# Three seven-product units in each gate/up chunk, and a weight sum made by an adding transfer

## The chip, the core and the metric

The kernel runs on one core of a Trainium2 chip. The metric is device time in microseconds of one execution, the median of several; the profile is of one further execution and gives times from the start of its span. The engines are TensorE (PE; its weight loads are shown as PEld), VectorE (DVE), ScalarE (ACT), GpSimd (POOL) and SyncE (SP), which here only issues transfers.

## What is computed

One encoder block on 256 tokens of width 2048 in float32: a gated feed-forward network of width 5632, a mixing stage (sparse attention and a recurrent time mix between two projections), a second network, a last norm. The change lies in the two networks:

```python
def swiglu(x, w_gate, w_up, w_down):
    return (jax.nn.silu(x @ w_gate) * (x @ w_up)) @ w_down

h = h + 0.5 * swiglu(rms_norm(h, ffn1_norm[l]), ffn1_w_gate[l], ffn1_w_up[l], ffn1_w_down[l])
...
h = h + 0.5 * swiglu(rms_norm(h, ffn2_norm[l]), ffn2_w_gate[l], ffn2_w_up[l], ffn2_w_down[l])
```

## The kernel before

**Products.** Each float32 factor is split into a high and a low part, and a product is three matmuls: high by high, high by low, low by high. Weights come in groups of 256 rows by 512 columns (512 KB). For a group, SP loads it into one of four slots of `raw` (`load_group`, L382), ScalarE copies the high part to `whi` (`split_hi`, L396), VectorE subtracts to get the low part in `wlo` (`split_lo`, L404), and PE multiplies it with two blocks of 128 tokens: 2 x 2 x 3 = 12 matmuls with 512 columns (`project_tokens`, L419). `whi` and `wlo` have four slots as well. The load of group g waits until group g-4 has been split by both engines; a split waits until PE has used group g-4.

**Units.** Two groups together, of the gate and of the up matrix (or of two column blocks of the down matrix), make a 2 x 2 by 2 x 2 block product, which needs seven products instead of eight: 21 matmuls instead of 24 (`unit_products`, L433). For that VectorE makes sums of the raw weights in `col_sum` (`unit_sums`, L786): four additions of 128 x 512, one of which replaces the first half of the up group in its raw slot by the sum of its two halves. ScalarE and VectorE split the sums (`unit_hi`, `unit_lo`), and PE takes first the gate group, then the up group, then the sums. `col_sum` and its low part share one buffer, so the sums of a unit wait until PE has finished the unit before (`unit_used`); in the down stage the raw sums have a buffer of their own. Sums of token blocks are made once for each network, beside its first chunk (`halves_dve`, `halves_hi`, `halves_lo`).

**Gate/up stage.** Each network has eleven chunks of 512 columns (`FC`), of 16 groups each. The first has no units. In each of the other ten the order of the groups is written out in `CHUNK` (L47): gate groups into psA, up groups into psB, two units between them; shared partial products of the units go to psT and psM. When they are done, ScalarE copies one share out, VectorE adds the shares (`close_gate`, L929: four instructions on 128 x 512 and one on 128 x 1024), and ScalarE applies silu to psA (`silu_gate`, L702), all near the end of the same chunk. PE may begin the next chunk when silu has read psA. Product of gate and up (`gate_up`, L901), a transpose by quads through DRAM (`turn_quads`, `quads_store`, `quads_load`) and its split (`turned_hi`, `turned_lo`) follow during the next two chunks. SP stores the quads ahead of group 11 and reads them back ahead of group 13.

**Down stage.** Two pairs of column blocks, each with 44 groups; seven units in each pair (seven and eight in the second network), with two plain groups between two units, 14 or 6 plain groups ahead of the first and 4, 10 or 12 behind the last (`down_order`, L83). The same `unit_sums` serves it.

Every engine runs its instructions in the written order. POOL issues some small loads of parameters at the start (L2699), and in the mixing stage it clears three buffers (`mix_pool`, L1236).

Of the kernel before, what the change touches and what calls it, by code (L numbers as in the profile page):

```python
# [19 lines left out]
ALU = mybir.AluOpType  # L20
# [23 lines left out]

GATE_UNITS = 2
GATE_PAIR = 2
CHUNK = ([("gate", j) for j in (0, 1, 4, 5)] + [("unit", 0)] + [("gate", j) for j in (6, 7)] + [("up", 0)] + [("unit", 1)]  # L47
         + [("up", j) for j in (1, 4, 5, 6, 7)])
UNITS = ((7, 7), (7, 8))
# [108 lines left out]
def build(nc, a, out):  # L158
    with ExitStack() as ctx:
# [128 lines left out]
        x_sum_hi = at("x_sum_hi", [P, 3, GATE_UNITS, P], consts, plus=4 * P + 12 * P * GATE_UNITS, dt=F32R)  # L288
        shares = at("shares", [P, TB, COLS], consts, plus=4 * P + 24 * P * GATE_UNITS)
        xl_sum = at("xl_sum", [P, KD, S], xl)  # L290
# [62 lines left out]
        act_lo_ready = sem("act_lo_ready")  # L353
        col_step = sem("col_step")
        col_hi_ready = sem("col_hi_ready")
        col_lo_ready = sem("col_lo_ready")
# [119 lines left out]
        def squares_act(f, c):  # L476

            if f == 0:
                nc.scalar.wait_ge(x_landed[c], 16)
            else:  # L480
                nc.scalar.wait_ge(x_added, DC * (f - 1) + c + 1)
            if f == 2 and c == 0:
                stored(nc.scalar, "pv", 1)
            for tb in range(TB):
                dump = (silu[:, tb, :] if f == 0 else psT[:, tb * COLS:(tb + 1) * COLS] if f == 2 or c == DC - 1
                        else shares[:, tb, :])
# [214 lines left out]
        def ffn_act(f, base, first_act):  # L701
            def silu_gate(n):  # L702
# [12 lines left out]
                last.then_inc(silu_ready, 1)  # L715

            def turned_hi(n):

                nc.scalar.wait_ge(quads_landed, n * 16 + 16 * (f * FC + 1))
                for tb in range(TB):  # L720
                    last = nc.scalar.copy(turned_tokens(hh, n, tb), landed[:, tb])
                last.then_inc(hh_ready, 1)

            def first_chunk():
                for j in range(PER):
                    if j >= SLOTS:
# [4 lines left out]
                    if j == PER - 2:  # L731
                        halves_hi(xh, xl_sum, x_sum_hi, x_sum, GATE_PAIR // 2, sum_number(f))

            def chunk(n):
                for kind, j, g in chunk_items():
                    split_hi(base, n, PER, g)
                    if kind == "unit":
                        unit = FIRST_UNIT[f] - GATE_UNITS + j
                        nc.scalar.wait_ge(col_step, n * (4 * GATE_UNITS) + (4 * unit + 2))
                        split_hi(base, n, PER, g + 1)  # L740
                        unit_hi(n, unit)
                    if g == PER - 2:

                        nc.scalar.wait_ge(quads_stored, n * 64 + 64 * f * FC)
                        nc.scalar.wait_ge(unit_used, n * GATE_UNITS + FIRST_UNIT[f])
                        nc.scalar.copy(silu[:, 0, :], Q1).then_inc(share_copied, 1)
                silu_gate(n)
                turned_hi(n - 1)
            first_chunk()
# [6 lines left out]
            for i, (m, kind, part, j, g) in enumerate(down_items(f)):  # L756
                split_hi(down, 0, 0, g)
                if kind == "unit":
                    nc.scalar.wait_ge(col_step, 4 * unit + 2)
                    split_hi(down, 0, 0, g + 1)  # L760
                    unit_hi(0, unit, col_raw)
                    unit += 1
                if i == GD + SLOTS:
                    turned_hi(FC - 1)
# [14 lines left out]
        def unit_hi(n, unit, col_sum=col_sum):  # L779

            nc.scalar.wait_ge(col_step, n * (4 * GATE_UNITS) + (4 * unit + 4))
# [32 lines left out]
        def batch(b, f):  # L814

            if f is None:
                return 2, slice(0, 2)
            n = min(2, max(UNITS[f]) - 2 * b)
# [81 lines left out]
        def ffn_dve(f, base, first_dve):  # L900
# [40 lines left out]
            def first_chunk():  # L941
                for j in range(PER):
                    if j >= SLOTS:
                        split_lo(base, 0, PER, j)
                    first_dve(j)
                    if j == PER - 3:
                        nc.vector.wait_ge(group_used, base + GD + GATE_PAIR + GATE_UNITS)
                        halves_dve(xh, xl, xl_sum, x_sum, GATE_PAIR // 2, sum_number(f))
                    if j == PER - 1:
                        halves_lo(xh, xl, xl_sum, x_sum_lo, x_sum_hi, x_sum, GATE_PAIR // 2, sum_number(f))  # L950

            def chunk(n):
                for kind, j, g in chunk_items():
                    if kind == "unit":
                        unit = FIRST_UNIT[f] - GATE_UNITS + j
                        unit_sums(base, n, PER, g, unit)
                        split_lo(base, n, PER, g)
# [4 lines left out]
                    else:  # L962
                        split_lo(base, n, PER, g)
                    if g == 1 and not (isinstance(n, int) and n == 1):
                        turned_lo(n - 2)
                    if g == SLOTS - 1:
# [10 lines left out]
            for i, (m, kind, part, j, g) in enumerate(down_items(f)):  # L977
                if kind == "unit":
                    if unit == FIRST_UNIT[f] + GATE_TOTAL:
                        nc.vector.wait_ge(unit_used, unit)  # L980
                    unit_sums(down, 0, 0, g, unit, col_raw)
                    split_lo(down, 0, 0, g)
# [3 lines left out]
                else:  # L986
                    split_lo(down, 0, 0, g)
                if i == 1:
                    turned_lo(FC - 2)
# [26 lines left out]
            if f == 1:  # L1016
                gain_dve(2)

        def add_down(f, down, c):
# [47 lines left out]
        def ffn_pe(f, base):  # L1067
# [22 lines left out]
            def chunk(n):  # L1090

                nc.tensor.wait_ge(silu_ready, n + f * FC)
                for i, (kind, j, g) in enumerate(chunk_items()):
                    if kind == "gate":
                        project_tokens(psA, xh, xl, base, n, PER, g, j * KT, i == 0, False)
                    elif kind == "up":
                        project_tokens(psB, xh, xl, base, n, PER, g, j * KT, j == 0, j == GD - 1, open_half=0)
                    else:
# [335 lines left out]
        def stored(eng, name, i):  # L1434
# [16 lines left out]
        vector_step = sem("vector_step")  # L1451
        count = {}

        def done(ins, name):

            if name in steps:
                ins.then_inc(steps[name], 1)
# [4 lines left out]
        def need(eng, name):  # L1462

            eng.wait_ge(steps[name], 1)

        def after(name):

            if name in steps:
                nc.vector.wait_ge(steps[name], 1)
# [1230 lines left out]
        def _(pool):  # L2700
# [7 lines left out]
            for row, col_, name in ((0, 0, "rwkv_mu_w"), (0, 64, "rwkv_mu_a"), (1, 0, "rwkv_mu_g"), (1, 64, "rwkv_mu_g")):  # L2708
                pool.dma_start(prow2[row:row + 1, col_:col_ + 64], a[name].rearrange("(o n) -> o n", o=1))\
                    .then_inc(const_landed, 16)  # L2710
            mix_pool(pool)

        @block.scalar
# [152 lines left out]
```

## Time and profile before

| | |
|---|---|
| median of 3 runs | 1834.93 us (1834.79 to 1837.94) |
| span of the profiled execution | 1834.2 us |
| PE busy | 1819.6 us, 99%, 10696 matmuls |
| DVE busy | 1505.4 us, 82% |
| ACT busy | 995.2 us, 54% |
| POOL busy | 11.1 us, 1% |
| bytes moved | 380.36 MB, 207 GB/s over the span |

Matmuls are pipelined: a row's duration is longer than the distance to the next row, and the distance is what a matmul costs. On VectorE and ScalarE, too, a row's duration is a little longer than the distance between neighbours that don't wait. A number in brackets at the end of a timeline row is the idle time before it, with what ended it. The first network lies in about the first 630 us of the span, the mixing stage after it up to about 1080 us, then the second network.

### The profile page before, as it was taken

How to read it: one execution, taken by the hardware profiler on the slowest of the kernel's cores; microseconds unless marked ns; L12 is line 12 of the kernel's file. 1: busy time of each engine (PE TensorE's matmuls, PEld its weight loads, DVE VectorE, ACT ScalarE, POOL GpSimd, SP SyncE). 2: the span in 40 equal slices, each digit the busy share in tenths (PEclk: the TensorE clock that was granted, in tenths of full speed). 3: DMA queues.
4: the chain of work that ended last, by engine and by line, in shares of the span. 5: the costliest groups of instructions: out<-in, count | busy, mean ns of one | idle time of the engine just before them, and what ended most of it. 6: DMA issues, size and time to landing. Idle time of an engine off the chain costs nothing. (4 is left out here: it accounts for less than half of the span.)

```text
span 1834.2 us, 29749 instructions
## 1 busy us (share of the span) xinstructions
PE 1819.6 (99%) x10696; PEld 1546.4 (84%) x10696; DVE 1505.4 (82%) x1755; ACT 995.2 (54%) x1181; POOL 11.1 (1%) x23
## 2 busy tenths in 40 slices
PE   9999999999999999999999999999999999999998
PEld 7888888888888888999998878888888888888886
DVE  5888888888988985788867866688888888889996
ACT  7555555545555655754535655545555555555554
POOL 1000000000000000000000000000000000000000
PEclk9999999999999999999999999999999999999999
DMA  7677666777766778564443557677777677676664
GB/s 252 221 219 228 219 216 215 220 229 236 233 202 204 225 224 267 173 184 140 138 116 106 176 171 261 180 232 231 229 224 232 216 227 222 217 240 195 209 208 157
DMA packets 207851, 380.36 MB, mean 207 GB/s; under 512 B 16016, under 2 KB 35728, under 8 KB 207504
## 3 DMA queue, kind: packets, MB, share of 16 engines
q1 hardware_dynamic: 206768, 377.08, 65.7%
q10 hardware_dynamic: 480, 1.97, 0.3%
q8 instruction: 61, 1.00, 0.2%
q14 instruction: 30, 0.25, 0.0%
q0 software_dynamic: 512, 0.06, 0.0%
HBM read 360.19 MB, written 18.87 MB: 207 GB/s over the span
## 5 line engine op out<-in xcount | busy, mean ns | idle before, releaser
L402 ACT CAST whi<-raw 128x1024 fp32r<-128x1024 f32 (+1 forms) x648 | 675.1, 1047 | 700.8 <-DVE raw L1476 189.6
L411 DVE TENSOR_TENSOR wlo<-raw,whi 128x1024 fp32r<-128x1024 f32 (+1 forms) x648 | 771.7, 1212 | 208.4 <-ACT whi L402 194.5
L428 PE MATMUL psA<-whi,xh 128*128 128x512 f32 (+1 forms) x572 | 219.5, 384 | 0.5 <-DVE wlo L411 0.5
L428 PE MATMUL psA<-whi,xl 128*128 128x512 f32 (+1 forms) x572 | 219.2, 383 | 0.0
L428 PE MATMUL psA<-wlo,xh 128*128 128x512 f32 (+1 forms) x572 | 219.1, 383 | 0.0
L428 PE MATMUL psB<-whi,xh 128*128 128x512 f32 x544 | 211.7, 389 | 0.0
L428 PE MATMUL psB<-wlo,xh 128*128 128x512 f32 x544 | 211.6, 389 | 0.0
L428 PE MATMUL psB<-whi,xl 128*128 128x512 f32 x544 | 211.6, 389 | 0.0
L428 PEld LDWEIGHTS psA<-whi,xh 128*128 128x128 f32 x572 | 107.4, 188 | 21.6 <-DVE wlo L411 0.7
L428 PEld LDWEIGHTS psA<-whi,xl 128*128 128x128 f32 x572 | 107.4, 188 | 21.2
L428 PEld LDWEIGHTS psA<-wlo,xh 128*128 128x128 f32 x572 | 107.4, 188 | 21.0
L428 PEld LDWEIGHTS psB<-whi,xl 128*128 128x128 f32 x544 | 102.1, 188 | 21.3
L428 PEld LDWEIGHTS psB<-whi,xh 128*128 128x128 f32 x544 | 102.1, 188 | 21.1
L428 PEld LDWEIGHTS psB<-wlo,xh 128*128 128x128 f32 x544 | 102.1, 188 | 21.1
L1252 PE MATMUL psB<-xh,whi 128*128 128x256 f32 x320 | 92.7, 290 | 0.5 <-DVE wlo L411 0.5
L428 PE MATMUL psA<-whi,hh 128*128 128x512 f32 x236 | 91.8, 389 | 0.0
L428 PE MATMUL psA<-wlo,hh 128*128 128x512 f32 x236 | 91.8, 389 | 0.0
L428 PE MATMUL psA<-whi,hl 128*128 128x512 f32 x236 | 91.8, 389 | 0.0
L1252 PE MATMUL psB<-xh,wlo 128*128 128x256 f32 x320 | 90.5, 283 | 0.0
L1252 PE MATMUL psB<-xl,whi 128*128 128x256 f32 x320 | 90.4, 283 | 0.0
L428 PE MATMUL psB<-whi,hh 128*128 128x512 f32 x220 | 85.7, 390 | 0.0
L428 PE MATMUL psB<-whi,hl 128*128 128x512 f32 x220 | 85.6, 389 | 0.0
(520 smaller groups left out, 3447.3 us busy)
## 6 DMA issues: line engine op xcount, KB each, us to landing
raw<-in_ffn_w_gate SPq DMA_DIRECT2D x176, 512.0 KB, 4.5
raw<-in_ffn_w_up SPq DMA_DIRECT2D x176, 512.0 KB, 4.6
raw<-in_ffn_w_down SPq DMA_DIRECT2D x176, 512.0 KB, 4.6
raw<-in_w_in SPq DMA_DIRECT2D x80, 512.0 KB, 3.6
raw<-in_w_out SPq DMA_DIRECT2D x32, 512.0 KB, 4.2
quads_dram<-stage SPq DMA_DIRECT2D x88, 128.0 KB, 4.2
stage<-quads_dram SPq DMA_DIRECT2D x22, 512.0 KB, 4.3
x<-in_x SPq DMA_DIRECT2D x4, 512.0 KB, 7.5
```

Source lines behind the costliest of these rows:

```text
L402: nc.scalar.copy(whi[:, slot, :, 0:ncol], raw[:, slot, :, 0:ncol]).then_inc(hi_ready, 1)
L411: nc.vector.tensor_tensor(wlo[:, slot, :, 0:ncol], raw[:, slot, :, 0:ncol], whi[:, slot, :, 0:ncol].bitcast(F32), ALU.subtract).then_inc(l ...
L428: mm = nc.tensor.matmul(ps[:, tb, 0:ncol], lhs[:, k0 + t, tok], rhs[:, slot, t, 0:ncol], start=(first and t == 0 and p == 0 and tb != open ...
L1252: mm = nc.tensor.matmul(ps[:, i * S:(i + 1) * S], w[:, slot, t, ct * P:(ct + 1) * P], h[:, k0 + t, :], start=(first and t == 0 and p == 0 ...
```

## The change

A gate/up chunk gets three units instead of two (gate and up rows 2, 3 and 4 of eight), and its order is rewritten: two plain groups between the first unit and the second, one between the second and the third, three behind the third. In all units, those of the down stage too, the sum of the up group's two halves is no longer a VectorE instruction: POOL issues a transfer that reads the second half of the group from DRAM again and adds it to the first half in the raw slot (256 KB, `accum_op`), after the group has landed and after the unit before had its transfer; VectorE's sums and ScalarE's split of the up group wait for it. VectorE's remaining three sums are rearranged. The closing sums of a chunk, with the copy of the share and silu, move behind the first split of the next chunk (in the last chunk, behind the first split of the down stage), and `turned_hi` moves behind the second. `shares` moves into the buffer of `col_sum`. Two groups of four semaphores of the mixing stage become one counted semaphore each.

```diff
-GATE_UNITS = 2
+GATE_UNITS = 3
 GATE_PAIR = 2
-CHUNK = ([("gate", j) for j in (0, 1, 4, 5)] + [("unit", 0)] + [("gate", j) for j in (6, 7)] + [("up", 0)] + [("unit", 1)]
-         + [("up", j) for j in (1, 4, 5, 6, 7)])
+CHUNK = ([("gate", j) for j in (0, 1, 5, 6)] + [("unit", 0), ("gate", 7), ("up", 0), ("unit", 1), ("up", 1), ("unit", 2)]
+         + [("up", j) for j in (5, 6, 7)])
...
+            def copy_share(n):
+
+                nc.scalar.wait_ge(quads_stored, n * 64 + 64 * f * FC)
+                nc.scalar.wait_ge(unit_used, n * GATE_UNITS + FIRST_UNIT[f])
+                nc.scalar.copy(silu[:, 0, :], Q1).then_inc(share_copied, 1)
...
             def chunk(n):
                 for kind, j, g in chunk_items():
                     split_hi(base, n, PER, g)
+                    if g == 0 and not (isinstance(n, int) and n == 1):
+                        copy_share(n - 1)
+                        silu_gate(n - 1)
+                    if g == 1 and not (isinstance(n, int) and n == 1):
+                        turned_hi(n - 2)
                     if kind == "unit":
                         unit = FIRST_UNIT[f] - GATE_UNITS + j
-                        nc.scalar.wait_ge(col_step, n * (4 * GATE_UNITS) + (4 * unit + 2))
+                        wait_summed(nc.scalar, n, unit)
                         split_hi(base, n, PER, g + 1)
                         unit_hi(n, unit)
-                    if g == PER - 2:
-
-                        nc.scalar.wait_ge(quads_stored, n * 64 + 64 * f * FC)
-                        nc.scalar.wait_ge(unit_used, n * GATE_UNITS + FIRST_UNIT[f])
-                        nc.scalar.copy(silu[:, 0, :], Q1).then_inc(share_copied, 1)
-                silu_gate(n)
-                turned_hi(n - 1)
...
+        def wait_summed(eng, n, unit):
+
+            eng.wait_ge(up_summed, n * (16 * GATE_UNITS) + 16 * (unit + 1))
+
+        def sum_rows(pool, n, unit, pair, w, col, base, per, g):
+
+            wait_raw(pool, base + g + 1, n, per)
+            if not (isinstance(n, int) and n * GATE_UNITS + unit == 0):
+                pool.wait_ge(up_summed, n * (16 * GATE_UNITS) + 16 * unit)
+            second = w[(pair * KT + 1) * P:(pair * KT + 2) * P, :]
+            pool.dma_start(raw[:, (base + g + 1) % SLOTS, 0, :], second[:, bass.ds(col, COLS)], accum_op=ALU.add)\
+                .then_inc(up_summed, 16)
+
         def unit_sums(base, n, per, g, unit, col_sum=col_sum):
 
             gate, up = (base + g) % SLOTS, (base + g + 1) % SLOTS
-            steps = n * (4 * GATE_UNITS)
+            steps = n * (3 * GATE_UNITS)
             wait_raw(nc.vector, base + g, n, per)
-            wait_raw(nc.vector, base + g + 1, n, per)
...
-            tt(col_sum[:, 0, :], raw[:, gate, 0, :], raw[:, up, 0, :], ALU.add).then_inc(col_step, 1)
-            nc.vector.wait_ge(col_step, steps + (4 * unit + 1))
-            tt(raw[:, up, 0, :], raw[:, up, 0, :], raw[:, up, 1, :], ALU.add).then_inc(col_step, 1)
-            tt(col_sum[:, 1, :], col_sum[:, 0, :], raw[:, up, 1, :], ALU.add).then_inc(col_step, 1)
-            nc.vector.wait_ge(col_step, steps + (4 * unit + 3))
+            tt(col_sum[:, 1, :], raw[:, gate, 0, :], raw[:, up, 0, :], ALU.add).then_inc(col_step, 1)
+            nc.vector.wait_ge(col_step, steps + (3 * unit + 1))
+            tt(col_sum[:, 0, :], col_sum[:, 1, :], raw[:, up, 1, :], ALU.subtract).then_inc(col_step, 1)
             tt(col_sum[:, 2, :], col_sum[:, 1, :], raw[:, gate, 1, :], ALU.add).then_inc(col_step, 1)
...
             def chunk(n):
                 for kind, j, g in chunk_items():
                     if kind == "unit":
                         unit = FIRST_UNIT[f] - GATE_UNITS + j
+                        wait_summed(nc.vector, n, unit)
                         unit_sums(base, n, PER, g, unit)
...
+                    if g == 0 and not (isinstance(n, int) and n == 1):
+                        close_gate(n - 1)
                     if g == 1 and not (isinstance(n, int) and n == 1):
                         turned_lo(n - 2)
...
-                    if g == PER - 2:
-                        close_gate(n)
...
                 if kind == "unit":
                     if unit == FIRST_UNIT[f] + GATE_TOTAL:
                         nc.vector.wait_ge(unit_used, unit)
+                    wait_summed(nc.vector, 0, unit)
                     unit_sums(down, 0, 0, g, unit, col_raw)
```

## Rows read from the trace of the kernel before

**Rows 1.** The page: busy us, share, instructions; slices of the span in tenths.
```profile
PE 1819.6 (99%) x10696; PEld 1546.4 (84%) x10696; DVE 1505.4 (82%) x1755; ACT 995.2 (54%) x1181; POOL 11.1 (1%) x23
...
PE   9999999999999999999999999999999999999998
...
PEclk9999999999999999999999999999999999999999
```

**Rows 2.** Stretches: length; busy us of PE, PEld, DVE, ACT, POOL; clock, DMA share, GB/s.
```profile
309.11:351.27 42.16, 42.16 (x187) 34.92 (x186) 35.97 (x38) 22.29 (x23) 0.00 (x0) 1.00 0.71 225
478.00:620.00 142.00, 142.00 (x628) 117.64 (x627) 129.57 (x157) 77.52 (x82) 0.00 (x0) 1.00 0.68 213
...
1826.00:1834.00 8.00, 0.86 (x4) 0.38 (x2) 2.32 (x6) 2.26 (x5) 0.00 (x0) 0.71 0.59 221
```

**Rows 3.** Timeline of PE: start, duration; starts of two chunks, then of two down units.
```profile
309.11 0.39 PE L428 MATMUL psA<-whi,xh 128*128 128x512 f32 x1
309.34 0.39 PE L428 MATMUL psA<-wlo,xh 128*128 128x512 f32 x1
...
351.27 0.39 PE L428 MATMUL psA<-whi,xh 128*128 128x512 f32 x1
...
515.83 0.39 PE L439 MATMUL psT<-whi,hh 128*128 128x512 f32 x1
...
526.03 0.39 PE L439 MATMUL psT<-whi,hh 128*128 128x512 f32 x1
```

**Rows 4.** Timeline of DVE around the chunk that PE begins at 309.11.
```profile
303.40 1.23 DVE L411 TENSOR_TENSOR wlo<-raw,whi 128x1024 fp32r<-128x1024 f32 x1 [1.01 <-ACT whi L402]
...
314.18 0.68 DVE L1476 TENSOR_TENSOR col_sum<-raw 128x512 f32<-128x512 f32 x1
...
316.83 2.35 DVE L411 TENSOR_TENSOR wlo<-raw,whi 128x1024 fp32r<-128x1024 f32 x2
319.10 1.75 DVE L1476 TENSOR_TENSOR col_lo<-col_sum,col_hi 128x1536 fp32r<-128x1536 f32 x1
...
327.57 0.69 DVE L1476 TENSOR_TENSOR col_sum<-raw 128x512 f32<-128x512 f32 x1 [2.12 <-DMA raw<-in_ffn_w_up]
...
339.87 0.69 DVE L1476 TENSOR_TENSOR shares<-psM,stage 128x512 f32<-128x512 f32 x1
...
342.51 1.22 DVE L1476 TENSOR_TENSOR shares<-psT,shares 128x1024 f32<-128x1024 f32 x1
```

**Rows 5.** Timeline of ACT in the same chunk: a split; silu and what follows.
```profile
315.69 1.05 ACT L402 CAST whi<-raw 128x1024 fp32r<-128x1024 f32 x1 [2.60 <-DVE raw L1476]
...
342.51 1.27 ACT L714 ACTIVATE stage<-psA,ss 128x512 f32<-128x512 f32 x2 [0.87 <-DVE psA L1476]
343.67 1.14 ACT L721 CAST hh<-stage 128x512 f32 x2
```

**Rows 6.** SP's queue: two issues; landing of L389's loads, 309 to 351.
```profile
318.21 0.37 SPq L389 DMA_DIRECT2D raw<-in_ffn_w_up  x1
319.40 0.37 SPq L389 DMA_DIRECT2D raw<-in_ffn_w_gate  x1
...
DMA to landing us min/median/max: 3.7/4.6/6.1
```

**Rows 7.** Transfers of the whole run: KB each, median us from issue to landing.
```profile
raw<-in_ffn_w_down SPq DMA_DIRECT2D x176, 512.0 KB, 4.6
...
out<-x SPq DMA_DIRECT2D x8, 256.0 KB, 2.5
...
lora_g<-in_rwkv_g ACTq DMA_DIRECT2D x2, 256.0 KB, 4.4
...
prow<-in_mix_norm POOLq DMA_DIRECT2D x1, 8.0 KB, 5.3
```

**Rows 8.** Timeline of DVE in the down stage: first sums of a unit.
```profile
510.07 0.69 DVE L1476 TENSOR_TENSOR col_raw<-raw 128x512 f32<-128x512 f32 x1
...
539.53 0.69 DVE L1476 TENSOR_TENSOR col_raw<-raw 128x512 f32<-128x512 f32 x1 [0.73 <-DMA raw<-in_ffn_w_down]
```

More of the change, by code:

```diff
@@ L288, in build @@
         x_sum_hi = at("x_sum_hi", [P, 3, GATE_UNITS, P], consts, plus=4 * P + 12 * P * GATE_UNITS, dt=F32R)
-        shares = at("shares", [P, TB, COLS], consts, plus=4 * P + 24 * P * GATE_UNITS)
+        shares = at("shares", [P, TB, COLS], col_sum)
+        dump_at = at("dump_at", [P, TB, COLS], consts, plus=4 * P + 12 * COLS)
         xl_sum = at("xl_sum", [P, KD, S], xl)
@@ L354, in build @@
         col_step = sem("col_step")
+        up_summed = sem("up_summed")
         col_hi_ready = sem("col_hi_ready")
@@ L485, in squares_act @@
                 dump = (silu[:, tb, :] if f == 0 else psT[:, tb * COLS:(tb + 1) * COLS] if f == 2 or c == DC - 1
-                        else shares[:, tb, :])
+                        else dump_at[:, tb, :])
                 nc.scalar.activation(dump, x[:, tb, c * COLS:(c + 1) * COLS], ACT.Square,
@@ L730, in first_chunk @@
                         silu_gate(0)
-                    if j == PER - 2:
+                    if j == PER - 1:
                         halves_hi(xh, xl_sum, x_sum_hi, x_sum, GATE_PAIR // 2, sum_number(f))
@@ L758, in ffn_act @@
                 if kind == "unit":
-                    nc.scalar.wait_ge(col_step, 4 * unit + 2)
+                    wait_summed(nc.scalar, 0, unit)
                     split_hi(down, 0, 0, g + 1)
@@ L762, in ffn_act @@
                     unit += 1
+                if i == 0:
+                    copy_share(FC - 1)
+                    silu_gate(FC - 1)
+                if i == 1:
+                    turned_hi(FC - 2)
                 if i == GD + SLOTS:
@@ L779, in unit_hi @@
         def unit_hi(n, unit, col_sum=col_sum):
-            nc.scalar.wait_ge(col_step, n * (4 * GATE_UNITS) + (4 * unit + 4))
+            nc.scalar.wait_ge(col_step, n * (3 * GATE_UNITS) + (3 * unit + 3))
             if not (isinstance(n, int) and n * GATE_UNITS + unit == 0):
@@ L816, in batch @@
             if f is None:
-                return 2, slice(0, 2)
+                return GATE_UNITS, slice(0, GATE_UNITS)
             n = min(2, max(UNITS[f]) - 2 * b)
@@ L945, in first_chunk @@
                     first_dve(j)
-                    if j == PER - 3:
+                    if j == PER - 2:
                         nc.vector.wait_ge(group_used, base + GD + GATE_PAIR + GATE_UNITS)
                         halves_dve(xh, xl, xl_sum, x_sum, GATE_PAIR // 2, sum_number(f))
-                    if j == PER - 1:
-                        halves_lo(xh, xl, xl_sum, x_sum_lo, x_sum_hi, x_sum, GATE_PAIR // 2, sum_number(f))
             def chunk(n):
@@ L963, in chunk @@
                         split_lo(base, n, PER, g)
+                    if g == 0 and not (isinstance(n, int) and n == 1):
+                        close_gate(n - 1)
                     if g == 1 and not (isinstance(n, int) and n == 1):
                         turned_lo(n - 2)
+                    if g == 1 and isinstance(n, int) and n == 1:
+                        halves_lo(xh, xl, xl_sum, x_sum_lo, x_sum_hi, x_sum, GATE_PAIR // 2, sum_number(f))
                     if g == SLOTS - 1:
                         gate_up(n - 1)
-                    if g == PER - 2:
-                        close_gate(n)
             first_chunk()
@@ L987, in ffn_dve @@
                     split_lo(down, 0, 0, g)
+                if i == 0:
+                    close_gate(FC - 1)
                 if i == 1:
@@ L1017, in ffn_dve, with ffn_pool, chunk @@
                 gain_dve(2)
+        def ffn_pool(pool, f, base, w_up, w_down):
+            def chunk(n):
+                for kind, j, g in chunk_items():
+                    if kind == "unit":
+                        sum_rows(pool, n, FIRST_UNIT[f] - GATE_UNITS + j, GATE_PAIR + j, w_up, n * COLS, base, PER, g)
+            chunk(1)
+            with pool.Fori(2, FC) as n:
+                chunk(n)
+            unit = FIRST_UNIT[f] + GATE_TOTAL
+            for m, kind, part, j, g in down_items(f):
+                if kind == "unit":
+                    sum_rows(pool, 0, unit, j, w_down, (2 * m + 1) * COLS, base + FC * PER, 0, g)
+                    unit += 1
         def add_down(f, down, c):
@@ L1092, in chunk @@
                 nc.tensor.wait_ge(silu_ready, n + f * FC)
+                first_up = next(j for kind, j in CHUNK if kind == "up")
                 for i, (kind, j, g) in enumerate(chunk_items()):
@@ L1096, in chunk @@
                     elif kind == "up":
-                        project_tokens(psB, xh, xl, base, n, PER, g, j * KT, j == 0, j == GD - 1, open_half=0)
+                        project_tokens(psB, xh, xl, base, n, PER, g, j * KT, j == first_up, j == GD - 1, open_half=0)
                     else:
@@ L1447, in build @@
             "kr_out", "k_roped", "qi_roped", "q_packed0", "q_packed1", "q0_roped", "q1_roped", "q_back0", "q_back1",
[2 rows of a table removed]
+            "scored0", "scored1", "scored2", "scored3", "max0", "max1", "max2", "max3", "exp",
+            "recip", "shares0", "shares1", "shares2", "shares3",
             "att_hi0", "att_hi1")}
@@ L1452, in build @@
         count = {}
+        counted = {f"{name}{n}": (name, n + 1) for name in ("exp", "recip") for n in range(4)}
         def done(ins, name):
-            if name in steps:
+            if name in counted:
+                ins.then_inc(steps[counted[name][0]], 1)
+            elif name in steps:
                 ins.then_inc(steps[name], 1)
@@ L1462, in need @@
         def need(eng, name):
-            eng.wait_ge(steps[name], 1)
+            name, level = counted.get(name, (name, 1))
+            eng.wait_ge(steps[name], level)
         def after(name):
-            if name in steps:
+            if name in counted:
+                nc.vector.wait_ge(steps[counted[name][0]], counted[name][1])
+            elif name in steps:
                 nc.vector.wait_ge(steps[name], 1)
@@ L2710, in _ @@
                     .then_inc(const_landed, 16)
+            ffn_pool(pool, 0, 0, *ffn1[1:])
             mix_pool(pool)
+            ffn_pool(pool, 1, base2, *ffn2[1:])
         @block.scalar
```

2 rows, old and new, of the table steps are left out of this document.

## The prediction, made before the changed kernel was run

> **What bounds the kernel now.** I read the page's busy shares and slices first, then the busy time of two stretches, then the timelines of PE, VectorE, ScalarE and the SP queue inside one gate/up chunk, last the transfers. PE is busy 99% of the span, in every slice, at the full granted clock [rows 1]. In the gate/up chunk that runs from 309.11 to 351.27 PE never pauses: 42.16 us busy of 42.16, VectorE 35.97, ScalarE 22.29 [rows 2]. Matmuls follow each other every 0.227 us (309.11, 309.34), and one chunk begins 42.16 us after the last [rows 3]: 12 plain groups of 12 matmuls and two units of 21 are 186 matmuls. So a chunk is bound by PE's matmul count alone; a group costs 2.72 us, a unit 4.76 us for two groups. In the down stage it is the same: unit starts lie 10.20 us apart, one unit and two plain groups [rows 3].
>
> What the reader must see next is how little stands between this and another bound. The ring of raw weights has four slots; the load of group g waits until g-4 is split. VectorE finishes the first split of the chunk at 304.63 (303.40 and 1.23), PE wants it at 309.11, so the lead is 4.5 us [rows 3, 4]; ahead of the second unit VectorE already stands 2.12 us still for a load [rows 4], and in the down stage its sums wait for a load too [rows 8].
>
> **What is removed.** Per chunk three matmuls: 183 x 0.2267 = 41.48 us, 0.68 less, in 20 chunks 13.6 us. This is the only work that leaves PE; the down stage keeps its matmuls. VectorE loses one sum per unit: the four sums fill 314.18 to 316.83, 2.65 us [rows 4], so three take 2.0. Its third unit adds 2.0 of sums and 1.67 of low halves (the 1.75 row, less the overlap of neighbours); with 2 x 0.65 off, a chunk is 35.97 + 2.4 = 38.3 us of 41.48. VectorE's throughput does not become the bound. ScalarE gains one 1.4 us copy at 22 of 42 us: hidden, and hidden still if the chunk shortens.
>
> **What is added, and on which path.** The sum of the up rows moves from VectorE, where it followed the landing at once, into a transfer issued by POOL, which must wait for the landing, is issued, reads the rows again, adds, lands; VectorE then begins its sums. VectorE is in order: behind its new wait stand the splits of the unit's gate and up groups, hence the slots' release, hence the next loads of SP. ScalarE's split of the up group waits as well, with the high copy behind it. I call the price of the transfer, from issue to landing, T. The lines of the diff for the down units add the same wait there.
>
> No row shows an adding transfer. The nearest: a plain 256 KB store, 2.5 us with little else moving; a 256 KB load for lora_g, 4.4 us; POOL's own small transfers, 5.3 us, at a time when the engines were crowded [rows 7]. Bounds: 2.5 below (a gain below nothing is excluded, a step that wasn't there can't land before it is issued), above 5.3 plus 0.7 for the bytes, 6.0. I take 4.4, the row of the same size and direction. The Trainium skill (DMA: Bandwidth & Descriptors, "Anatomy of one DMA — SWDGE (gpsimd) path") gives a fixed 2.0 us and bytes over 436 GB/s for POOL's transfers; that would be T = 2.6, an estimate by that page; POOL's 5.3 us for 8 KB here disagree, in a crowded stretch [rows 7].
>
> **The slot's turn.** From the end of one unit's second split to the end of the next unit's in the same slot: to SP's issue 0.15 (the first of two splits ended at about 318.06, issue 318.21 [rows 4, 6]), load L, POOL's and VectorE's wake 0.1 each, T, sums 2.0, two splits 2.3 [rows 4]. That is L + T + 4.65. For L the loads of the chunk took 3.7 at least and 4.6 in the median [rows 6]; of those on this path some go out alone and some behind another, so 4.2.
>
> A chunk after the change has this cycle, all in the order of the queues: group 1 to group 5 (unit 0's up rows), one turn; 5 to 9 (unit 1's), one turn; group 8, split 1.15 earlier, to group 12 (unit 2's), one turn less 1.15; group 12 to the next chunk's group 0, a plain refill of L + 2.55 (0.15, a wake of 0.1, ScalarE's split 1.05, hand-over 0.1, VectorE's 1.15 [rows 4, 5]); then the closing sums, now behind that first split. They hold up group 1: four of the five sums 2.64 (339.87 to 342.51 [rows 4]), silu on ScalarE 1.16 (342.51 to 343.67 [rows 5]), ScalarE's split of group 1, 1.05, VectorE's 1.15, hand-overs 0.3, together 6.3. Sum: 4L + 3T + 21.65. With 4.2 and 4.4 it is 16.8 + 13.2 + 21.65 = 51.65 us against 41.48 of PE: the ring is the new bound. Against 42.16 each chunk loses 9.49 us, 20 chunks 190, less the lead of 4.5 us that each network begins with: 181.
>
> Moving the closing sums by itself is covered: PE wants silu only three plain groups (8.16 us) after the last unit, and copy 0.57, sums 2.64 and silu 1.16 take about 4.7 with hand-overs. If the cover were gone it would cost at most those 4.7 us a chunk; in the cycle above it is counted. SP's stores and load of the turned quads stay at groups 11 and 13, where SP waits longer for splits than for them: nothing. The larger token sums in the first chunk, half as much work again, and the moved low halves lie beside the first chunk's matmuls: nothing to 2 us per network.
>
> **Down stage.** A turn now: VectorE starts its sums every 9.82 us on average (510.07 to 539.53, three turns [rows 8]), just under PE's 10.20, and the load at 4.6 [rows 7] accounts for it: 0.15 + 4.6 + 0.1 + 2.65 + 2.3 = 9.8. After: 9.25 + T = 13.65. 25 gaps between units lose 3.45 each, 86 us; the first units of the four strings, with four plain groups (10.9) ahead of them, 2.75 each, 11; less a lead of 4.5 four times, 18: 79 us.
>
> **Sum.** The profiled span is 1834.2 and the median of the runs 1834.93, 0.7 around it. 1834.9 + 181 + 79 = 2095 us.
>
> **Rivals.** (a) *Faster: PE's 0.68 us count, T is hidden.* 1834.9 - 13.6 = 1821. It decides below 4L + 3T + 21.65 = 41.48, that is T = 1.0 at L = 4.2 and 1.7 at 3.7; every row in [rows 7] speaks against it. A second thing speaks against it even at T = 0: unit 2 follows unit 1 after one plain group (2.72 us), and its sums share one buffer with unit 1's, so they wait for unit 1's last product; sums 2.0, split 1.15 and hand-overs 0.2 are 3.35, a pause of 0.63, which eats the 0.68. Chance 0.03.
> (b) *No change*, T small and that pause cancelling the gain: 1835, chance 0.04.
> (c) *Slower by a third of it: the transfer is quick.* With T = 2.5, at L = 4.2, a chunk is 45.95 (20 x 3.79 - 9 = 67) and a down turn 11.75 (39 + 3 - 18 = 24): 1926. The 2.5 us store [rows 7] speaks for it, POOL's 5.3 against. Chance 0.24. The page of the Trainium skill named above, with its 2.6, would give about this, an estimated 1935.
> (d) *Much slower*: T = 6.0 and L = 4.6, loads and adds in each other's way: chunk 58.05 (20 x 15.89 - 9 = 309), down turn 15.25 (126 + 17 - 18 = 125): 2269. The granted clock, 1.00 through all of this, is 0.71 in the last 8 us, where PE has nearly stopped, so part of them at 1.2 GHz [rows 2]; pauses of several us in a chunk could bring that and would lengthen PE's own part. Chance 0.14.
> My forecast, 1990 to 2180, has 0.55: T from about 3.2 to 5.4 at 89 us for each 1 us.
>
> **Range.** Lowest by the bounds, T = 2.5 and L = 3.7 (4.2 in the down stage): 43.95 a chunk, 27 us, and 13 for the down stage: 1875. Highest 2269. Between them lie the forecast, (c) and (d); outside (a), (b) and the tails. About 0.2% (3.7 us) is what a measurement of this kernel tells from no change: faster 0.03, same 0.04, slower 0.93.
>
> **What would show it.** Right: PE pauses in each gate/up chunk ahead of the units' splits, the chunk near 52 us; VectorE's first sum of a unit ended by the adding transfer, its issue-to-landing near 4.4 us; unit starts in the down stage near 13.7 us apart; loads not slower than now; the mixing stage between the two networks unchanged in length. Wrong: chunks of 42 us with VectorE's wait ended elsewhere (T hidden, so the slots are free earlier than I have it), or chunks that stretch while the adds land within 3 us (then a queue's order, or the clock, and not T). The weakest number is T: each 1 us of it moves the total by 3 x 20 + 29 = 89 us, one for each unit.

## The result, and the profile after

The changed kernel takes 2317.12 us in the median (2309.64 to 2319.55) against 1835.76 before, measured beside it: a ratio of 1.262, 95% interval 1.259 to 1.264. The direction is as forecast; the loss, 481 us, is nearly twice the 260 us forecast and lies above the top of the range. The profiled execution has a span of 2314.0 us. The page after, first busy time and slices (against [rows 1]), then the chain that ended last:

```profile
PE 1972.1 (85%) x10636; PEld 1624.1 (70%) x10636; DVE 1530.2 (66%) x1766; ACT 1009.3 (44%) x1201; POOL 88.3 (4%) x112
...
PE   9788878778797878999999998888878888887877
...
PEclk9988998989898999999999998889899999988999
...
DMA 21%; DVE 7%; PE 7%; issue 6%; ACT 2%; DVEq 0%; ACTq 0%; POOLq 0%; SPq 0%
```

Sixty matmuls are gone (10696 before), as the change says. But PE is no longer busy in every slice, VectorE's share has fallen from 82% to 66%, and the chain runs through transfers for 21% of the span. The slices also show where nothing happened: the middle, the mixing stage, is full as before. Its last projection, the matmuls of one tile with first and last start, takes as long in both kernels, 100.8 and 100.9 us (the first row is of the kernel before, the second of the changed one):

```profile
L428 PE MATMUL psB<-whi,mix_hi x64: 389/389/580, 1029.6 to 1130.4; 128*128 128x512 f32 x64
```

```profile
L430 PE MATMUL psB<-whi,mix_hi x64: 389/389/580, 1264.1 to 1365.0; 128*128 128x512 f32 x64
```

The first matmuls of the down stages (the first start in each row) say in which stages the time went. The first two rows are the first network's, before and after; the other two are the second's:

```profile
L428 PE MATMUL psA<-whi,hh x120: 389/389/389, 477.8 to 656.6; 128*128 128x512 f32 x120
```

```profile
L430 PE MATMUL psA<-whi,hh x120: 389/389/500, 642.4 to 878.7; 128*128 128x512 f32 x120
```

```profile
L428 PE MATMUL psA<-whi,hh x116: 389/389/389, 1597.1 to 1773.7; 128*128 128x512 f32 x116
```

```profile
L430 PE MATMUL psA<-whi,hh x116: 389/389/395, 1997.4 to 2236.8; 128*128 128x512 f32 x116
```

The first down stage begins 165 us later than before, the mixing stage's last projection 235, the second down stage 400, and the span ends 480 later. So the gate/up chunks of the two networks lose 165 and 166 us, the first down stage with the mixing stage 70 (2 of them in the mixing stage), the second down stage 80: 330 and 150, where 181 and 79 were forecast. (The mixing stage lies later than is said above: before the change the first down stage's matmuls end at 707 us and the mixing stage's at 1131.) Who waited for whom in the changed kernel (total us, times, longest):

```profile
DVE col_sum L1523 <- DMA raw<-in_ffn_w_up: 363.8, 60, 8.2
...
PE psT L441 <- DVE wlo L413: 325.7, 89, 6.7
...
DVE col_raw L1523 <- DMA raw<-in_ffn_w_down: 176.2, 27, 8.9
```

VectorE's first sum waits at every unit of the chunks, 60 times, and PE waits once for each of the 89 units, always at a unit's first product, for VectorE's low half of its gate group. The transfers (KB, median us from issue to landing; then least, median and most of the 89 adding ones), against [rows 7]:

```profile
raw<-in_ffn_w_gate SPq DMA_DIRECT2D x176, 512.0 KB, 4.7
raw<-in_ffn_w_up SPq DMA_DIRECT2D x176, 512.0 KB, 4.2
...
raw<-in_ffn_w_up POOLq DMA_DIRECT2D x60, 256.0 KB, 6.1
...
DMA to landing us min/median/max: 4.5/6.0/7.9
```

So T, which I took as 4.4 us, is 6.0. One cycle of the ring, read along the path that the prediction names. SP's issues, the landings of the first load in each of these four rows, then POOL's issues, then VectorE (start, duration):

```profile
350.54 0.37 SPq L391 DMA_DIRECT2D raw<-in_ffn_w_up  x1
...
365.42 4.35 SPq L391 DMA_DIRECT2D raw<-in_ffn_w_up  x2
...
380.66 0.40 SPq L391 DMA_DIRECT2D raw<-in_ffn_w_up  x1
...
394.39 7.80 SPq L391 DMA_DIRECT2D raw<-in_ffn_w_gate  x5
```

```profile
DMA to landing us min/median/max: 3.4/3.4/3.4
...
DMA to landing us min/median/max: 4.6/4.6/4.6
...
DMA to landing us min/median/max: 3.9/3.9/3.9
...
DMA to landing us min/median/max: 4.7/4.7/4.7
```

```profile
354.93 0.86 POOL L807 DMA_DIRECT2D raw<-in_ffn_w_up  x1 [26.24 <-DMA raw<-in_ffn_w_up]
370.70 0.86 POOL L807 DMA_DIRECT2D raw<-in_ffn_w_up  x1 [14.91 <-DMA raw<-in_ffn_w_up]
385.20 0.86 POOL L807 DMA_DIRECT2D raw<-in_ffn_w_up  x1 [13.63 <-DMA raw<-in_ffn_w_up]
```

```profile
349.19 1.22 DVE L413 TENSOR_TENSOR wlo<-raw,whi 128x1024 fp32r<-128x1024 f32 x1 [1.10 <-PE psB L430]
...
360.98 0.69 DVE L1523 TENSOR_TENSOR col_sum<-raw 128x512 f32<-128x512 f32 x1 [4.50 <-DMA raw<-in_ffn_w_up]
...
377.37 0.69 DVE L1523 TENSOR_TENSOR col_sum<-raw 128x512 f32<-128x512 f32 x1 [6.97 <-DMA raw<-in_ffn_w_up]
...
389.87 0.69 DVE L1523 TENSOR_TENSOR col_sum<-raw 128x512 f32<-128x512 f32 x1 [5.40 <-DMA raw<-in_ffn_w_up]
...
400.37 1.23 DVE L413 TENSOR_TENSOR wlo<-raw,whi 128x1024 fp32r<-128x1024 f32 x1 [1.13 <-ACT whi L404]
401.51 0.68 DVE L1523 TENSOR_TENSOR shares<-psM,stage 128x512 f32<-128x512 f32 x1
...
406.49 1.23 DVE L413 TENSOR_TENSOR wlo<-raw,whi 128x1024 fp32r<-128x1024 f32 x1 [1.10 <-ACT whi L404]
```

Group 1 is split from 349.19 on, the next chunk's group 1 from 406.49 on: 57.3 us. Between them: the load of unit 0's up rows goes out at 350.54 and POOL issues the adding transfer at 354.93 (4.4 us), VectorE starts its sums at 360.98 (6.05); unit 1: 365.42, 370.70 (5.3), 377.37 (6.7); unit 2: 380.66, 385.20 (4.5), 389.87 (4.7); the refill of the next chunk's group 0 goes out at 394.39 and is landed 4.7 us later; then the closing sums and silu hold group 1 up. These are 18.9 us that begin with a load, 17.4 that begin with an addition, and 21.0 for the rest.

But the 18.9 hold more than the loads: they landed after 3.4, 4.6, 3.9 and 4.7 us, 16.6 together, and POOL's row begins 1.0, 0.7 and 0.6 us after the landing that it waits for, 2.3 together. The additions landed after 5.8, 6.5 and 4.6 us, 16.9 together, and VectorE's three wakes are the other 0.4. The sum in the prediction had 16.8 for the loads, 0.3 for POOL's hand-over, 13.2 for the additions, 0.3 for VectorE's wakes and 21.05 for the rest. So the cycle has the terms that were forecast, and it is the addition and POOL's hand-over that are longer. It is the same in other chunks: over sixteen of them, worked out from the same rows, the means are 16.6, 2.2, 18.2, 0.4 and 21.06. Nine chunks of the first network, from the first closing sum (110.12) to the tenth (635.87), give 58.4 us each.

### The profile page after: what moved, and what is told of

Its sections match the earlier page's. It is cut to its first block and busy times, and to the rows that moved or that the text cites. A ratio compares the mean times of both kernels' runs of the same rounds, so it can differ in the third digit from the quotient of the medians.

```text
span 2314.0 us, 30169 instructions
## 1 busy us (share of the span) xinstructions
PE 1972.1 (85%) x10636; PEld 1624.1 (70%) x10636; DVE 1530.2 (66%) x1766; ACT 1009.3 (44%) x1201; POOL 88.3 (4%) x112
## 5 line engine op out<-in xcount | busy, mean ns | idle before, releaser
L1523 DVE TENSOR_TENSOR col_sum<-raw 128x512 f32<-128x512 f32 x60 | 41.5, 692 | 363.8 <-DMA raw<-in_ffn_w_up 363.8
L441 PE MATMUL psT<-whi,xh 128*128 128x512 f32 x60 | 39.4, 656 | 226.8 <-DVE wlo L413 226.8
L430 PE MATMUL psA<-wlo,xh 128*128 128x512 f32 (+1 forms) x492 | 188.5, 383 | 0.0
L430 PE MATMUL psA<-whi,xl 128*128 128x512 f32 (+1 forms) x492 | 188.5, 383 | 0.0
L430 PE MATMUL psB<-whi,xh 128*128 128x512 f32 x464 | 180.9, 390 | 0.0
L430 PE MATMUL psB<-wlo,xh 128*128 128x512 f32 x464 | 180.5, 389 | 0.0
L430 PE MATMUL psB<-whi,xl 128*128 128x512 f32 x464 | 180.5, 389 | 0.0
L795 ACT CAST col_hi<-col_sum 128x1536 fp32r<-128x1536 f32 x60 | 88.4, 1473 | 65.6 <-DVE col_sum L1523 65.6
L807 POOL DMA_DIRECT2D raw<-in_ffn_w_up x60 | 52.0, 867 | 1501.7 <-DMA raw<-in_ffn_w_up 1458.4
L1523 DVE TENSOR_TENSOR col_lo<-col_sum,col_hi 128x1536 fp32r<-128x1536 f32 x60 | 105.1, 1751 | 0.0
```

Of the source, the lines that this page charges most:

```text
L430: mm = nc.tensor.matmul(ps[:, tb, 0:ncol], lhs[:, k0 + t, tok], rhs[:, slot, t, 0:ncol], start=(first and t == 0 and p == 0 and tb != open ...
L441: mm = nc.tensor.matmul(into, lhs, rhs, start=(start and p == 0), stop=(stop and p == 2))
L807: pool.dma_start(raw[:, (base + g + 1) % SLOTS, 0, :], second[:, bass.ds(col, COLS)], accum_op=ALU.add)\
L1523: return V.tensor_tensor(out, a0, a1, op)
```

## The experiments

The chunk below is the distance of the closing sums, the mean of nine in the first network.

**Without the adding transfer.** VectorE makes the sum again, all else as changed.

```diff
-                        wait_summed(nc.vector, n, unit)
...
+            tt(raw[:, up, 0, :], raw[:, up, 0, :], raw[:, up, 1, :], ALU.add).then_inc(row_summed, 1)
+            nc.vector.wait_ge(row_summed, n * GATE_UNITS + (unit + 1))
             tt(col_sum[:, 1, :], raw[:, gate, 0, :], raw[:, up, 0, :], ALU.add).then_inc(col_step, 1)
```

> The changed kernel with the one adding transfer per unit taken out: VectorE makes the sum of the up group's halves again (a fourth instruction per unit), everything else as changed: three units per gate/up chunk, closing sums behind the next chunk's first split. Theory (the turn of a raw slot, load + adding transfer + sums + splits, sets the pace, and only the transfer is too long): the chunk goes back from 58.4 us to about 43 to 44 (41.5 of PE, plus the pause of 0.6 to 1.3 us ahead of unit 2, whose sums wait for unit 1), the down stage to its length before, in all 1850 to 1880 us, clock 1.00. Rival A (three units or the moved closing sums make the chunk long): 2100 to 2200 us, since only the down stage, 150 us, comes back.

Measured 1880.35 us, ratio 1.024 (1.022 to 1.025), clock 0.999, chunk 44.2 us (272.28 to 316.30 for one). So 437 of the 481 us are the adding transfer's, and three units with moved closing sums lose 44 us by themselves. Two rows of that run, VectorE's and PE's waits:

```profile
304.16 0.69 DVE L1501 TENSOR_TENSOR raw<-raw 128x512 f32<-128x512 f32 x1 [1.83 <-PE psA L441]
```

```profile
PE psT L441 <- DVE wlo L413: 34.5, 39, 1.4
```

The first sum of unit 2 waits 1.83 us for PE to finish unit 1: rival (a)'s second objection, seen. PE pauses up to 1.4 us, about twice a chunk, and the 0.68 us saved is gone more than once.

**Adding transfers in the down stage alone.**

```diff
+            if col_sum is not col_raw:
+                tt(raw[:, up, 0, :], raw[:, up, 0, :], raw[:, up, 1, :], ALU.add).then_inc(row_summed, 1)
...
-                        wait_summed(nc.vector, n, unit)
...
-                    wait_summed(nc.vector, 0, unit)
+                    wait_added(nc.vector, downs(f, unit))
```

> Adding transfers in the down stage alone; in the gate/up chunks VectorE makes the sum, with three units and moved closing sums as changed. Theory: the two stages lose independently of each other; the chunks as in the run without any adding transfer (44.2 us), the down stage as in the changed kernel, unit starts 15.2 us apart, 29 turns: 1880 + 150 = 2030 us. If the sum of the parts does not hold (2030 missed by more than 20 us), the stages act on each other.

Measured 2030.32 us; chunk 44.2, unit starts in the down stage 15.3 us apart (536.76 to 628.53, six gaps). The stages add up: 150 us in the down stages, the other 287 of the transfer's 437 us in the chunks.

**Two units instead of three, transfer and moved closing kept.**

```diff
-GATE_UNITS = 3
+GATE_UNITS = 2
...
+CHUNK = ([("gate", j) for j in (0, 1, 4, 5)] + [("unit", 0)] + [("gate", j) for j in (6, 7)] + [("up", 0)] + [("unit", 1)]
+         + [("up", j) for j in (1, 4, 5, 6, 7)])
```

> The changed kernel with the old number and order of units, two in a gate/up chunk; adding transfer and moved closing sums stay. Theory: two turns of a slot with the transfer in them instead of three on the path: about 52 us a chunk at a transfer of 6 us, so 20 x 6 us less than changed, about 2180 us, the down stage as changed (unit starts 15.2 us apart). Rival A (the third unit itself is what costs): near 1990 us, only the down stage's 150 us remaining.

Measured 2233.22 us, chunk 54.6 us: the rival falls, but my 2180 us missed too. A turn taken away gave 3.8 us a chunk, not 6. Rows of ScalarE in that run show what I had left out:

```profile
372.63 1.06 ACT L404 CAST whi<-raw 128x1024 fp32r<-128x1024 f32 x1 [2.65 <-PE psB L430]
375.35 1.05 ACT L404 CAST whi<-raw 128x1024 fp32r<-128x1024 f32 x1 [1.66 <-PE psB L430]
```

Behind its last unit this order has five plain groups, and there the splits wait for PE again, which is late by the unit's delay: that part of the path seems to go through PE and not through the ring. This is read from the rows; no run isolates it.

**The parts of the transfer's price.** Three runs change the transfer alone: half the width; a copy instead of an addition; and that copy from ScalarE's queue (in the down stages too, and without the wait for the unit before's transfer).

```diff
-            pool.dma_start(raw[:, (base + g + 1) % SLOTS, 0, :], second[:, bass.ds(col, COLS)], accum_op=ALU.add)\
+            pool.dma_start(raw[:, (base + g + 1) % SLOTS, 0, 0:COLS // 2], second[:, bass.ds(col, COLS // 2)], accum_op=ALU.add)\
```

> The changed kernel with adding transfers of half the width (256 of 512 columns, 128 KB; the sum of the other columns is left out). Its packets are half as long. Theory: about 2.0 us from issue to the first packet stay, the moving time of about 3.5 to 4 us falls; landing 4.5 to 5 instead of 6.0, and each 1 us is worth 3 x 20 + 29 = 89 us: 2190 to 2230 us. Rival (the price is all latency of the software queue): landing near 6, 2300 us. Rival (what costs is the wait's place in VectorE's order, not its length): no change.

```diff
+            pool.dma_start(raw[:, (base + g + 1) % SLOTS, 0, :], second[:, bass.ds(col, COLS)])\
```

> The changed kernel with the same transfers from the same queue, 256 KB each, but copying instead of adding (so the sum is left out: the first half is overwritten by the second). Theory: a packet of 2 KB takes about 85 ns as in the plain loads instead of about 178 ns, the moving time halves: landing about 4.3 us instead of 6.0, 1.7 x 89 = 150 us less, about 2165 us. Rival (the software queue alone costs, adding is free): landing 6, 2300 us.

```diff
                     if kind == "unit":
                         unit = FIRST_UNIT[f] - GATE_UNITS + j
+                        sum_rows(nc.scalar, n, unit, GATE_PAIR + j, w_up, n * COLS, base, PER, g)
                         wait_summed(nc.scalar, n, unit)
```

> As the run with plain copies of 256 KB (no adding, the sum left out), but issued from ScalarE's queue instead of POOL's, right after ScalarE's split of the unit's gate group. Theory: the software queue is a part of the price (about 2 us from issue to first packet); landing about 3.3 us instead of 4.8, 1.5 x 89 = 130 us less than the copies from POOL: about 2070 us. Rival (the queue makes no difference): 2205 us.

Measured 2231.19, 2204.72 and 2172.05 us. The copies landed after 4.8 us where I expected 4.3, and so took 40 us more than the 2165 expected. Landing of the transfers (KB, median), half width, copy, copy from the other queue:

```profile
raw<-in_ffn_w_up POOLq DMA_DIRECT2D x60, 128.0 KB, 5.1
```

```profile
raw<-in_ffn_w_up POOLq DMA_DIRECT2D x60, 256.0 KB, 4.8
```

```profile
raw<-in_ffn_w_up ACTq DMA_DIRECT2D x60, 256.0 KB, 4.6
```

Half the bytes save 0.9 us, no adding 1.2 us, and each is worth what 89 us for each 1 us says: 0.9 x 89 = 80 (86 measured), 1.2 x 89 = 107 (112 measured). The third run missed: I expected 3.3 us from a queue that is not POOL's, and it took 4.6 in the chunks and 4.8 in the down stages, in the mean of all 89 as long as from POOL, 4.85 us. So the queue did not change the landing here. The 33 us below the copy from POOL come from ahead of the transfer. One load of up rows in this run (SP's row, its landing) and ScalarE's row that issues the copy:

```profile
319.77 0.37 SPq L391 DMA_DIRECT2D raw<-in_ffn_w_up  x1
...
DMA to landing us min/median/max: 3.7/3.7/3.7
...
323.63 0.34 ACTq L807 DMA_DIRECT2D raw<-in_ffn_w_up  x1
```

The load lands at 323.47 and the copy goes out 0.16 us later; in the changed kernel POOL took 0.6 to 1.0 us for this step. The means, worked out from the traces of the two copy runs, are 0.14 us on ScalarE against 0.71 on POOL in the chunks, and 0.05 against 0.31 in the down stages: 41 us over 89 transfers, 33 measured.

**POOL does the addition itself**, so that the length of the step changes and every wait of VectorE and ScalarE stays.

```diff
+            slot = (base + g + 1) % SLOTS
+            pool.tensor_tensor(raw[:, slot, 0, :], raw[:, slot, 0, :], raw[:, slot, 1, :], ALU.add).then_inc(up_summed, 1)
```

> The changed kernel with the adding transfer replaced by one addition of 128 x 512 on POOL itself, after the landing; all waits, the order of the units and the three sums on VectorE stay as changed. So only the length of the step changes, from 6 us to about 1 to 1.5. Theory (4L + 3T + 21.65 a chunk, with loads at 4.4 and T = 1.3): 43.2 us a chunk, near the pause bound of 42.2; down turn below PE's 10.2; 1840 to 1865 us, clock 1.00. Rival (a wait on POOL at this place costs by itself, or POOL and VectorE hinder each other): over 1900 us.

Measured 1877.5 us, ratio 1.023 (1.021 to 1.024), chunk 43.9; a little above the 1865 expected. Of the 43 us that the span is longer than before, 31 lie in the chunks and 11 in the down stages, where none were expected. There the expectation went against the prediction's own sum: 9.25 + T is 10.7 us at T = 1.44, above PE's 10.2 and not below. The row (least, median and most ns):

```profile
L805 POOL TENSOR_TENSOR raw<-raw x89: 1279/1291/2267, 62.4 to 1833.2; 128x512 f32<-128x512 f32 x89
```

The step from the landing to the finished sum was 6.8 us in the chunks (6.1 and 0.7 of hand-over); now it is 1.5 (a mean of 1.44, and 0.07). The chunk lost 14.5 us by that, 2.8 for each 1 us, with the three waits still there: what costs is the step's length and not the place of the wait.

**Closing sums moved, two units**: the edit of the first run (VectorE makes the sum), the old number and order of units, closing sums moved. The rearranged sums, the new places of `shares` and the semaphores, and the larger token sums of the first chunk stay in it.

```diff
-GATE_UNITS = 3
+GATE_UNITS = 2
...
+CHUNK = ([("gate", j) for j in (0, 1, 4, 5)] + [("unit", 0)] + [("gate", j) for j in (6, 7)] + [("up", 0)] + [("unit", 1)]
+         + [("up", j) for j in (1, 4, 5, 6, 7)])
```

> No adding transfer, two units in the old order, and only the closing sums (with share copy, silu and the turned split) moved behind the next chunk's first split, as changed. Theory: the move is covered, 42.2 to 42.8 us a chunk, 1835 to 1850 us. Rival (the move is what makes the run without adding transfers 44 us slower than before): 1870 to 1880 us.

Measured 1843.9 us, ratio 1.004 (1.003 to 1.006), chunk 42.4: covered but for 8 us, for which no single wait of PE stands out.

**Units spread**: VectorE's sum, three units, two plain groups between any two; and the same with POOL's addition and silu behind ScalarE's second split. In both SP reads the quads back ahead of group 14, since no item begins at group 13 in this order.

```diff
+CHUNK = ([("gate", j) for j in (0, 1, 5, 6)] + [("unit", 0), ("gate", 7), ("up", 0), ("unit", 1), ("up", 1), ("up", 5), ("unit", 2)]
+         + [("up", j) for j in (6, 7)])
```

> No adding transfer, three units, closing moved, and two plain groups between any two units instead of two and one (so two instead of three behind the last). Theory: the pause ahead of the third unit, whose sums wait until PE has finished the second, goes (1.3 us a chunk), 42.5 to 43.3 us a chunk, 1845 to 1860 us. Rival (VectorE, now near 40 of 41.5 us, is the bound and the place of the units does not matter): 1880 us as in the run without adding transfers.

> As the one before, with two plain groups between any two units, and silu behind ScalarE's second split of the next chunk instead of its first. Theory: no pause ahead of the third unit, VectorE at 38.3 us of 41.5: 41.5 to 42.5 us a chunk, 1822 to 1842 us, the first form of the change that could beat the kernel before. Rival (the ring is still the bound, or POOL hinders VectorE): 1850 us or more.

Measured 1855.7 us (ratio 1.010, 1.009 to 1.012) and 1857.73 us (1.012, 1.010 to 1.014). The first is as expected: spreading the units brings 25 of the 44 us back. The second missed; a row of POOL and one of VectorE in it show why in the chunks:

```profile
343.25 1.29 POOL L805 TENSOR_TENSOR raw<-raw 128x512 f32<-128x512 f32 x1 [10.52 <-DMA raw<-in_ffn_w_up]
```

```profile
344.72 0.69 DVE L1520 TENSOR_TENSOR col_sum<-raw 128x512 f32<-128x512 f32 x1 [3.58 <-POOL raw L805]
```

VectorE, now with less to do, waits 3.58 us for unit 2's sum, which waits for the load. So in this chunk the ring sets the time even when the addition costs 1.3 us: 42.7 us a chunk in the first network, 42.4 in the second. But of the 23.5 us that the span is longer than before only 9.5 lie in the chunks and 13 in the down stages, where unit starts lie 10.5 us apart in the mean of 25 gaps, 10.0 before. A form with POOL's addition in the chunks alone was not run. None of these beats the kernel before.

## Why the prediction was right or wrong

- **What bounds it, and the direction: right.** PE was bound by its matmul count, and after the change the ring of four raw slots sets the pace: the run with POOL's short addition leaves VectorE's and ScalarE's waits in place and brings 440 of the 481 us back.
- **T: the step that failed.** "I take 4.4, the row of the same size and direction": a copy of 256 KB in this place does land in 4.8 us, so the row was near the mark for a copy, but adding costs 1.2 us more. 1.6 us too little at 89 us for each 1 us is 142 of the 222 us by which the sum fell short. I had taken a plain transfer's price for the value and left the adding itself unpriced; the bound above, 6.0, holds the measured value, though not for its reason, since a copy from POOL's queue lands no later than one from ScalarE's.
- **POOL's hand-over: the second term mis-sized.** The sum had 0.1 us from the load's landing to POOL's issue. It was 0.69 in the mean of the 60 transfers in the chunks and 0.31 in the 29 of the down stages, about 41 us in all; the copy run from ScalarE's queue bears it out with 33 us.
- **L: right.** 4.2 in the sum, 16.8 for four loads; 16.6 on the path read above and in the mean of sixteen chunks. The loads of the up rows became quicker at the median, 4.2 after against 4.6 before; those of the gate and down rows took 0.2 longer.
- **The rest of the cycle: right**, 21.0 in the chunk read, where 21.65 less the six wakes is 21.05. With L and T as measured the prediction's formula gives 16.6 + 16.9 + 21.65 = 55.2 for the chunk of 57.3; 2.0 of the 2.1 that are missing are POOL's hand-over.
- **Down stage: right in its turn, too low in its sum.** 9.25 + T = 15.25 with T = 6.0, and unit starts lie 15.3 us apart. Two of the gaps before the change were 7.5 us and not 10.2, since only one plain group stands there in the second network; the mean of the 25 gaps was 10.0. So they lose 5.3 us each, 133 together, and the first units 17: 150, as measured with the chunks left out and with them in. The leads that I took off (18 us here, 9 in the chunks) did not show: the chunks lost 330 us, and 20 times the lengthening of a chunk is 325. Why no lead was left is open.
- **What is left.** T, POOL's hand-over and the leads are 142 + 41 + 27 = 210 of the 222 us.
- **Rival (a), faster by hiding T: refuted** as its own objections said. With VectorE's sum, without any transfer, the third unit still loses; with the units spread it loses less, and the ring remains.
- **Moving the closing sums at nothing: off by up to 8 us**, from the run with two units and without the transfer. Other small parts of the change are left in it, so the 8 us need not all be the move's.
- **Rival (d)'s clock.** It fell, and its effect is bounded rather than measured by a run. PE after a long pause, then later in the same unit (start, duration, idle before), and the two stretches (length; busy us of PE, PEld, DVE, ACT, POOL; clock, DMA share, GB/s):

```profile
323.34 0.80 PE L441 MATMUL psT<-whi,xh 128*128 128x512 f32 x1 [6.74 <-DVE wlo L413]
323.94 0.63 PE L441 MATMUL psT<-wlo,xh 128*128 128x512 f32 x1
324.36 0.63 PE L441 MATMUL psT<-whi,xl 128*128 128x512 f32 x1
...
328.41 0.40 PE L441 MATMUL psM<-col_hi,x_sum_hi 128*128 128x512 f32 x1
328.64 0.39 PE L441 MATMUL psM<-col_lo,x_sum_hi 128*128 128x512 f32 x1
```

```profile
323.30:327.50 4.20, 4.16 (x10) 3.29 (x11) 3.93 (x3) 2.33 (x3) 0.00 (x0) 0.50 0.69 230
328.40:334.00 5.60, 4.94 (x22) 3.75 (x20) 1.40 (x3) 1.05 (x1) 0.29 (x1) 1.00 0.65 188
```

After 6.74 us of waiting the matmuls follow each other every 0.43 us and the granted clock is 0.50, the lower level, 1.2 GHz; from 328.4 on they follow every 0.23 us at 1.00. The granted clock of the whole run is 0.926. In the chunk read above PE's slower stretch is on the path only where VectorE's split of group 1 waits 1.10 us for PE at 349.19, and one chunk later that wait ends with ScalarE. So in these chunks the lower clock costs about 1 us at most; what it costs in all the others is not measured.

## What to carry to other kernels

A step put between a buffer's landing and its release is paid on the buffer's turn, however idle its engine is: count load, step, use and release once round the ring, compare it with what the consumer takes for as many groups, and only then ask which engine has time to spare. Here VectorE had 6 of 42 us free and PE needed only 0.68 us less, while three additions of 6 us were laid on a ring that had next to no room. And where no row shows an operation, a copy of the same size is its floor and not its price. The way from one transfer's landing to the issue of the next by another engine is a term of its own, here 0.7 us on POOL and 0.14 on ScalarE, and belongs in the turn.

## What the runs showed of the hardware

- An adding transfer keeps the engines busy about twice as long as a copy of the same bytes. Queue totals of the changed kernel and of the run with copies (packets, MB, share of 16 engines' span), with 89 transfers each and 512 small packets of parameters:

```profile
q0 software_dynamic: 13328, 23.40, 6.2%
```

```profile
q0 software_dynamic: 7632, 23.40, 3.0%
```

  6.2% of 16 x 2314 us is 25.8 us for each transfer, or 1.6 us on each of 16 engines; 3.0% of 16 x 2208 is 0.74. It also takes 144 packets instead of 80. On POOL the row that issues it lasts 0.87 us, and 0.54 for the copy.
- In this load the bytes were the smaller part of a landing: the networks' 512 KB loads took 4.2 to 4.8 us in the medians of the changed kernel, a 256 KB copy 4.6 to 4.8, an addition of 128 KB still 5.1. The Trainium skill (DMA: Bandwidth & Descriptors, "Anatomy of one DMA — SWDGE (gpsimd) path") gives 2.0 us and bytes over 436 GB/s, an estimate of 2.6 us for 256 KB; the measured 4.8 for a copy from POOL, beside other loads, decides against it here.
- From a load's landing to POOL's row that issues the next transfer it took 0.28 us in most of the down stages' units and about 0.7 in the chunks. There two more rows of POOL's sequencer, register operations and a move, stand in between (they start at 354.1 and 354.2 us, the transfer at 354.93). ScalarE issued in 0.14 us with the same two rows, so they are not the whole difference.
- POOL's own addition of 128 x 512 took 1.28 us at least and 2.27 at most. The Trainium skill (SBUF — State Buffer, "Who interferes with whom") says that VectorE instructions with two inputs in SBUF contend with a GpSimd instruction that reads there. The spread fits that; no run took VectorE away from it.
